# A projection with the contraction outermost, modulation products by 512 columns, and sums in column groups, in a one-core decoder step

## The chip, the core and the metric

The kernel runs on one core of one Trainium2 chip. The metric is the device time of one execution in microseconds, as the median of several runs. The engines meant below are PE (TensorE, matrix products), DVE (VectorE), ACT (ScalarE), POOL (GpSimd) and SP (SyncE, which here only issues DMAs).

## The reference

One decoder layer for a prompt of 256 tokens and 8 samples of 4 new tokens (288 token columns in all). The part that the change touches:

```
mod = (silu(c) @ w_ada + b_ada)            # 1024 x 6144, for 9 condition vectors
sh1, sc1, g1, sh2, sc2, g2 = mod
h = x * (1 + sc1) + sh1
qa, ka, va, qb, kb, vb, ga, gb = split(h @ w_in)   # 1024 x 5120
... rotary, two attention branches, gates, w_pa, w_pb ...
x = layer_norm(alpha * x + g1 * (merged @ w_o))
h2 = x * (1 + sc2) + sh2                    # then w_up, silu, w_down, layer_norm
```

All is float32. Each large product is done as three products of reduced-precision parts: weights and activations are split into a leading part (`hi`) and a rest (`lo`), and hi·hi, hi·lo and lo·hi are added in PSUM.

## The kernel before, in words

Features lie on partitions, and the 288 tokens are columns. A **unit** is 128 output features of one weight matrix: eight contraction blocks, three matmuls each, 24 matmuls of 288 columns into one PSUM bank (`unit_mm`). Two units share one weight load, 1 MB in one of three slots of a ring (`raw`, `RAW = 3`; transfer number n goes to slot n mod 3). ACT copies half a slot to `w_hi` (`split_hi`), DVE subtracts to get `w_lo` (`split_lo`), both four halves ahead of PE (`AHEAD = SPLIT = 4`). SP issues the transfers in order, and `free_slot(n)` makes it wait for what was in the slot: for a projection weight until its last `w_lo` half is made (`lo_ready`), for a piece of `w_ada` until PE has multiplied it (`ada_used`), since that one is read by PE straight from the ring.

A piece of `w_ada` is 256 columns with all eight contraction blocks (`ada_mm`, eight matmuls of 32 x 256 placed in four column groups of PE). Its product is copied by ACT to a row buffer (`ada_rows`), turned by PE (`ada_turn`) and added to the bias by DVE (`ada_add`).

**Opening:** eight pieces (shift and scale of the first sublayer) through the ring, then `h` is formed on DVE and split. **Mixing stage:** twelve rounds c = 0 to 11. In the ring the weights of round c are followed by one piece of `w_ada`; on PE the piece comes ahead of the two units of its round, and its turn behind them. The units alternate between two PSUM banks. After unit nb, ACT evicts the bank and then makes `w_hi` of half nb + 4; DVE shuffles the bank for the rotary embedding (which frees it, `acc_free`) and then makes `w_lo` of half nb + 4. PE waits for `acc_free` of the bank before it starts the next unit there. All these queues are in order.

Then key and value tiles are turned to token-major, the cached keys of the samples are transposed with three gate units between (`keys_turn`, `gate`), attention runs with the other gate units as filler, then `w_pa`/`w_pb`, `w_o`, LayerNorm, `w_up`, `w_down`. LayerNorm's sums are 16 products with a 128 x 128 matrix of 1/1024 (`ones_mm`), of xT and of its square, twelve of them between or behind the `w_o` units of the first six blocks and four at the end.

Of the kernel before, what the change touches and what calls it, by code (L numbers as in the profile page):

```python
# [36 lines left out]
SPLIT = 4  # L37
N_ADA0 = 8
MIX0 = N_ADA0
GATE0 = MIX0 + 24  # L40
# [75 lines left out]
C_END = C_SEL + SAMPLE  # L116


def constants():
# [12 lines left out]
    c[:, C_EPS] = EPS  # L132
    b, h, t = row_of(np.arange(128))
# [12 lines left out]
KV_PLACES = 7  # L146
# [10 lines left out]
ADA_FIRST = (0, 4, 1, 5, 2, 6, 3, 7)  # L157


def ada_chunk(n):  # L160

    if n < MIX0:
        return ADA_FIRST[n]
    if n < GATE0:
        return N_ADA0 + (n - MIX0) // 2 if (n - MIX0) % 2 else None
# [17 lines left out]
MIX_N = 12  # L183
# [27 lines left out]
def gate_slot(g):  # L211

    return ([12, 13, 14, 15, 24, 25, 26, 27, 28, 29, 30, 31, 16, 17, 22, 23])[g]
# [61 lines left out]
def build(nc, x_prompt, x_sample, cache_a, cache_rows, cache_b, page_table, c_prompt, c_sample, w_ada, b_ada, w_in,  # L275
# [24 lines left out]
    kvin, _ = sb("kvin", [128, 2, 6, 256])  # L300
# [7 lines left out]
    rowbuf, _ = sb("rowbuf", [128, 3, 256])  # L308
# [3 lines left out]
    rows, _ = sb("rows", [64, 128])  # L312
# [27 lines left out]
    k_early, _ = sb("k_early", [128, 6, 256], F32, o_qkvg + 24 * TOK * 4)  # L340
    k_late, _ = sb("k_late", [128, 6, 256], F32, o_tmp + 3 * 768 * 4)
# [3 lines left out]
    shift, _ = sb("shift", [128, TOK], F32, o_tmp)  # L345
    off_mean, _ = sb("off_mean", [128, TOK], F32, o_tmp + TOK * 4)
# [6 lines left out]
    st6, _ = sb("st6", [128, 3, 4, 6])  # L353
# [19 lines left out]
    c_zero, c_ready, ada_used, first_in = sem("c_zero"), sem("c_ready"), sem("ada_used"), sem("first_in")  # L373
# [21 lines left out]
    centred = sem("centred")  # L395
    centred_s, h2s_ready, pool_step, x1_scaled = (sem(n) for n in ("centred_s", "h2s_ready", "pool_step", "x1_scaled"))
# [29 lines left out]

    def raw_half(n_static_slot, hh, by_rows):

        if by_rows:
# [3 lines left out]
    def kv_place(b, kind):  # L433

        return (b % 4, b // 4) if kind == 0 else V_PLACE[b]

    def kv_tiles(b, kind, tile, n=1):

        place, _ = kv_place(b, kind)
        if place < 5:  # L440
# [11 lines left out]
    def part(t, slot, by_rows):  # L452
        if by_rows:
# [3 lines left out]
    def split_hi(act, nb, slot4, rslot, hh, need, by_rows=False):  # L457

        if isinstance(nb, int) and nb == 0:
            act.wait_ge(first_in, 16)  # L460
        else:
            act.wait_ge(raw_in[rslot], need)
# [10 lines left out]
    def halves(first, last):  # L473

        out = []
        for n in range(first, last):
            by_rows = PAB0 <= n < WO0 or n >= DOWN0
# [17 lines left out]

    PAB_BANK = (0, 1, 6, 3)
# [4 lines left out]
    SUMS_AFTER = {5: (0, 1), 6: (2, 3, 4), 7: (5,)}  # L501
# [1397 lines left out]
```

## Time and profile before

| | |
|---|---|
| runs, us | 570.57, 571.57, 565.12 (median 570.57) |
| profiled execution, us | 565.61 |
| its span on the core, us | 564.0 |
| granted TensorE clock, mean of the span | 0.966 |
| PE busy, us | 515.1 of 564.0 |
| bytes moved | 116.77 MB |

The profiled execution is about 5 us under the median of the three runs. Busy time of PE is the time in which a matmul is in flight. A granted clock of 1.00 is 2.4 GHz and 0.50 is 1.2 GHz. The kernel has a stretch of opening (to 42 us), the mixing stage (to 147 us), attention and gates (to about 280 us), output projection and LayerNorm (to about 335 us) and the feed-forward part.

### The profile page before, as it was taken

How to read it: one execution, taken by the hardware profiler on the slowest of the kernel's cores; microseconds unless marked ns; L12 is line 12 of the kernel's file. 1: busy time of each engine (PE TensorE's matmuls, PEld its weight loads, DVE VectorE, ACT ScalarE, POOL GpSimd, SP SyncE). 2: the span in 40 equal slices, each digit the busy share in tenths (PEclk: the TensorE clock that was granted, in tenths of full speed). 3: DMA queues.
4: the chain of work that ended last, by engine and by line, in shares of the span. 5: the costliest groups of instructions: out<-in, count | busy, mean ns of one | idle time of the engine just before them, and what ended most of it. 6: DMA issues, size and time to landing. Idle time of an engine off the chain costs nothing.

```text
span 564.0 us, 10305 instructions
## 1 busy us (share of the span) xinstructions
PE 515.1 (91%) x4047; PEld 473.5 (84%) x4047; DVE 289.5 (51%) x560; ACT 223.9 (40%) x376; POOL 91.9 (16%) x127
## 2 busy tenths in 40 slices
PE   3767999999999989999989979999999999999990
PEld 1537899989877979897889869999999999999980
DVE  0074657556643453354486586536555554335356
ACT  1053233334334454255543445455444434333311
POOL 1000113002860000000145052601111100000005
PEclk9977899999999999999899989999999999999995
DMA  8998599988086982183443363899776754354002
GB/s 278 336 286 261 186 368 343 344 274 278 8 279 204 287 285 76 47 278 131 150 150 116 110 224 113 286 333 305 248 272 221 254 191 159 128 200 163 24 1 84
DMA packets 96718, 116.77 MB, mean 207 GB/s; under 512 B 3595, under 2 KB 87755, under 8 KB 96164
## 3 DMA queue, kind: packets, MB, share of 16 engines
q1 hardware_dynamic: 94788, 102.74, 56.2%
q0 software_dynamic: 1888, 13.44, 6.7%
q8 instruction: 30, 0.49, 0.4%
q14 instruction: 12, 0.10, 0.1%
HBM read 112.89 MB, written 13.57 MB: 224 GB/s over the span
## 4 chain that ended last, share of the span: by engine, by line
PE 78%; DMA 11%; DVE 5%; ACT 2%; issue 1%; POOL 1%; SPq 1%; POOLq 0%; ACTq 0%; DVEq 0%
PE psum L654 20%; PE psum L656 19%; PE psum L655 19%; PE psum L679 4%; DMA raw<-in_w_in 4%; DMA raw<-in_w_up 3%; DMA raw<-in_w_ada 3%; PE psum L775 3%; PE psum L900 2%; PE psum L687 1%; PE psum L886 1%; PE psum L844 1%; PE psum L975 1%; PE psum L853 1%; PE psum L787 1%
## 5 line engine op out<-in xcount | busy, mean ns | idle before, releaser
L654 PE MATMUL psum<-act_hi,w_hi 128*128 128x288 f32 x736 | 224.1, 304 | 10.7 <-DVE act_lo L1625 3.9
L470 DVE TENSOR_TENSOR w_lo<-raw,w_hi 128x1024 fp32r<-128x1024 f32 x118 | 146.6, 1243 | 168.2 <-ACT w_hi L465 168.0
L655 PE MATMUL psum<-act_lo,w_hi 128*128 128x288 f32 x736 | 219.2, 298 | 0.0
L656 PE MATMUL psum<-act_hi,w_lo 128*128 128x288 f32 x736 | 218.5, 297 | 0.0
L465 ACT ACTIVATE w_hi<-raw 128x1024 fp32r<-128x1024 f32 x118 | 124.1, 1056 | 141.2 <-PE psum L656 92.6
L654 PEld LDWEIGHTS psum<-act_hi,w_hi 128*128 128x128 f32 x736 | 140.2, 191 | 19.0 <-issue 10.4
L655 PEld LDWEIGHTS psum<-act_lo,w_hi 128*128 128x128 f32 x736 | 140.5, 191 | 0.2
L656 PEld LDWEIGHTS psum<-act_hi,w_lo 128*128 128x128 f32 x736 | 140.7, 191 | 0.0
L654 PE MATMUL psum<-f_hi,w_hi 128*128 128x288 f32 x176 | 52.4, 298 | 0.6 <-DVE f_t L1663 0.6
L655 PE MATMUL psum<-f_lo,w_hi 128*128 128x288 f32 x176 | 51.9, 295 | 0.0
L656 PE MATMUL psum<-f_hi,w_lo 128*128 128x288 f32 x176 | 51.8, 294 | 0.0
L679 PE MATMUL psum<-raw,c_z 128*32 128x256 f32 x384 | 31.8, 460 | 7.0 <-DMA raw<-in_w_ada 7.0
L1767 POOL TENSOR_TENSOR qkvg<-qkvg,cst 128x288 f32 (+1 forms) x16 | 16.3, 1016 | 120.9 <-ACT qkvg L1134 120.9
L654 PEld LDWEIGHTS psum<-f_hi,w_hi 128*128 128x128 f32 x176 | 33.0, 187 | 0.9 <-issue 0.8
L656 PEld LDWEIGHTS psum<-f_hi,w_lo 128*128 128x128 f32 x176 | 33.1, 188 | 0.0
L655 PEld LDWEIGHTS psum<-f_lo,w_hi 128*128 128x128 f32 x176 | 33.0, 188 | 0.0
L1801 POOL TENSOR_TENSOR qkvg<-qkvg,gated 128x288 f32<-128x288 f32 x8 | 8.4, 1081 | 121.1 <-DVE gated L1580 121.1
L679 PEld LDWEIGHTS psum<-raw,c_z 128*32 128x32 f32 x384 | 11.5, 124 | 16.0 <-DMA raw<-in_w_ada 8.2
L1852 POOL DMA_DIRECT2D out<-in_cache_kv_a x24 | 11.7, 488 | 78.1 <-PE psum L656 76.5
L687 PEld LDWEIGHTS psum<-cst,rowbuf 128*128 128x128 f32 x96 | 15.2, 223 | 9.2 <-issue 4.9
L1298 ACT ACTIVATE silu_t<-psum 128x288 f32<-128x288 f32 x22 | 9.0, 408 | 33.3 <-PE psum L656 33.3
L1858 POOL TENSOR_TENSOR y_tok<-y_tok,ln_rows 128x512 f32<-128x512 f32 x2 | 3.4, 1702 | 104.3 <-ACT y_tok L1336 104.3
(180 smaller groups left out, 567.2 us busy)
## 6 DMA issues: line engine op xcount, KB each, us to landing
raw<-in_w_ada SPq DMA_DIRECT2D x24, 1024.0 KB, 7.4
raw<-in_w_up SPq DMA_DIRECT2D x22, 1024.0 KB, 6.2
raw<-in_w_in SPq DMA_DIRECT2D x19, 1024.0 KB, 7.2
raw<-in_w_down SPq DMA_DIRECT2D x10, 1024.0 KB, 4.9
out<-in_cache_kv_a POOLq DMA_DIRECT2D x16, 504.0 KB, 6.3
raw<-in_w_o SPq DMA_DIRECT2D x4, 1024.0 KB, 4.9
kvin<-in_cache_kv_a SPq DMA_DIRECT2D x8, 256.0 KB, 3.3
kvin<-in_cache_kv_b SPq DMA_DIRECT2D x16, 128.0 KB, 3.8
```

What stands on the lines that cost most here:

```text
L465: nc.scalar.activation(part(w_hi, slot4, by_rows), raw_half(rslot, hh, by_rows), ACT.Copy).then_inc(hi_ready, 1)
L470: nc.vector.tensor_tensor(part(w_lo, slot4, by_rows), raw_half(rslot, hh, by_rows), part(w_hi, slot4, by_rows).bitcast(F32), ALU.subtract) ...
L654: nc.tensor.matmul(out, hi_l, hi_r, start=start, stop=False, skip_group_check=True)
L655: nc.tensor.matmul(out, hi_l, lo_r, start=False, stop=False, skip_group_check=True)
L656: return nc.tensor.matmul(out, lo_l, hi_r, start=False, stop=stop, skip_group_check=True)
L679: mm = nc.tensor.matmul(psum[q:q + 32, bank, 0:256], c_z[:, k, :], raw8(slot)[:, k, :], start=(k < 4), stop=(k >= 4), skip_group_check=True)
L687: mm = nc.tensor.matmul(psum[:, ada_bank(i), 256 + 9 * hh:256 + 9 * hh + 9], rowbuf[:, i % 3, 128 * hh:128 * hh + 128], cst[:, C_ADA:C_ADA ...
L775: mm = nc.tensor.transpose(psum[:, bank, col:col + nr], kv_tiles(b, 0, tile)[0:nr, 0, 128 * hp:128 * hp + 128], cst[0:nr, 0:nr])
L900: mm = nc.tensor.matmul(psum[:, 6, E * i:E * i + E], prbT[:, u % 2, 128 * n:128 * n + 128], tok[:, kb, 1, 256 * g + E * h:256 * g + E * h ...
L1298: nc.scalar.activation(silu_t[:, q, :], psum[:, q, 0:TOK], ACT.Silu).then_inc(silu_ready, 1)
L1767: nc.gpsimd.tensor_tensor(block_at(qkvg, blk), block_at(qkvg, blk), cst[:, C_COS:C_COS + TOK], ALU.mult).then_inc(cos_done, 1)
L1852: pool.dma_start(kv_sample[g][bass.ds(b, 1), 0:BUF[g] - DEC_T, :], cache_rows[g][bass.ds(b, 1), DEC_T:BUF[g], :]).then_inc(moved, 16)
```

## The change

- **Opening.** `w_ada` is now taken by 512 columns and half the contraction (four matmuls of 32 x 512, one per column group), 1 MB as before; two such parts make a chunk, so there are 12 chunks and 24 parts. The first eight parts have five buffers of their own (`ada_s`), outside the ring. The order of chunks is 0, 2, 1, 3: shift and scale of the first 512 features come first.
- **First six units.** The units of blocks 12 to 17 (the values of the first branch) are computed together in six banks, contraction block by contraction block (`first_mm`: 18 matmuls for a block k). Their weights come as four transfers of two contraction blocks by 768 columns (0.75 MB) in the ring. Blocks 0 to 3 need only the first half of `h`, and the parts of chunks 1 and 3 are multiplied between them.
- **Mixing stage.** Nine rounds are left (`MIX_C`) and twelve parts of `w_ada`, in the order `MIX`: round 0, part, round 1, part, round 2, two parts, and so on by threes. PE takes rounds and parts in the order of the ring. Turns come once for two parts (96 turning products in all, as before).
- **Samples' keys.** Five of eight samples' keys are loaded before they are needed and not four, `keys_turn` runs in regular order with one `sample_scores` and one gate unit after turns 5, 9 and 13; gates take other slots.
- **LayerNorm sums.** For six of eight blocks the sums are made with a 128 x 32 matrix of 1/32 in four column groups (`quarter_sums`), evicted by ACT and DVE (`part_sum`), and gathered with two `ones_mm` (`gather_quarters`). Two blocks keep the old form.

```
+MIX_C = (0, 1, 2, 3, 4, 5, 9, 10, 11)
+MIX = [item for i in range(9) for item in [("w", i)] + [("a", m) for m in range(4 * i // 3, 4 * (i + 1) // 3)]]
+MIX0 = 4
+GATE0 = MIX0 + len(MIX)
+ADA_ORDER = (0, 2, 1, 3, 4, 5, 6, 7, 8, 9, 10, 11)
+START_BUF = (0, 1, 2, 3, 4, 0, 1, 2)
+    ROWS_AT = {2: 4, 3: 5, 5: 6, 6: 7, 8: 8}
...
             if m >= 0 and ada_chunk(m) is not None:
-                sp.wait_ge(ada_used, N_ADA_BEFORE[m] + 1)
+                sp.wait_ge(ada_used, N_ADA0 + N_ADA_BEFORE[m] + 1)
...
+        load_start(0)
...
+        load_start(1)
+        sp.dma_start(x_tok[:, 0:2, :], x_prompt.rearrange("a (t p) d -> p (a t) d", p=128)).then_inc(x_in, 16)
+        sp.dma_start(x_tok[0:SAMPLE, 2, :], x_sample.rearrange("b t d -> (b t) d")).then_inc(x_in, 16)
+        load_start(2)
+        load_start(3)
+        load_first(0)
+        load_first(1)
+        for q in range(4, N_ADA0):
+            load_start(q)
+        load_first(2)
+        load_first(3)
...
+    def first_mm(pe, k):
+
+        pe.wait_ge(lo_ready, k + 1)
+        pe.wait_ge(h_lo, k + 1)
+        for q in range(FIRST_N):
+            c = 128 * q
+            mm = mm3(psum[:, q, 0:TOK], w_hi[:, k % SPLIT, c:c + 128], w_lo[:, k % SPLIT, c:c + 128], act_hi[:, k, :], act_lo[:, k, :],
+                     k == 0, k == KT - 1)
...
-        for c in range(MIX_N):
+        first_mm(pe, 0)
+        first_mm(pe, 1)
+        ada_start(pe, 4)
+        first_mm(pe, 2)
+        ada_start(pe, 5)
+        first_mm(pe, 3)
+        ada_turn(pe, 2)
+        ada_start(pe, 6)
+        ada_start(pe, 7)
+        ada_turn(pe, 3)
+        for k in range(4, KT):
+            first_mm(pe, k)
+
+        to_turn = None
+        for n in range(MIX0, GATE0):
+            kind, m = MIX[n - MIX0]
+            if kind == "a":
+                ada_ring(pe, n)
+                if m % 2:
+                    to_turn = 4 + m // 2
+                continue
             for hh in range(2):
-                u = 2 * c + hh
-                if c >= 1 and hh == 0 or u == 1:
-                    ada_mm(pe, MIX0 + 2 * c + 1)
-                if c >= 1:
-                    pe.wait_ge(acc_free[hh], c)
-                unit_mm(pe, u, u % SPLIT, hh, h_lo if u == 0 else None)
-            ada_turn(pe, N_ADA0 + c)
+                nb = H_MIX + 2 * m + hh
+                pe.wait_ge(acc_free[hh], m + 1)
+                unit_mm(pe, nb, nb % SPLIT, hh)
+                if to_turn is not None:
+                    ada_turn(pe, to_turn)
+                    to_turn = None
...
+        for m, c in enumerate(MIX_C):
             for hh in range(2):
-                nb = H_MIX + 2 * c + hh
-                if c >= 1 and hh == 0:
-                    ada_rows(N_ADA0 + c)
+                nb = H_MIX + 2 * m + hh
+                if hh == 0 and ROWS_AT.get(m) is not None:
+                    ada_rows(ROWS_AT[m])
                 if c in ROPED:
                     act.wait_ge(half_used, nb + 1)
                     nc.scalar.activation(qkvg[:, 2 * c + hh, :], psum[:, hh, 0:TOK], ACT.Copy).then_inc(evicted, 1)
                 if nb + AHEAD < H_GATE + 2:
                     hi_static(act, nb + AHEAD)
...
+        def quarter_sums(first, last):
+            pe.wait_ge(squared, last)
+            for bank, src in ((4, xT), (5, qkvg[:, 8:16, :])):
+                for q in range(last - first):
+                    mm = nc.tensor.matmul(psum[32 * q:32 * q + 32, bank, 0:TOK], cst[:, C_W32:C_W32 + 32], src[:, SUM_ORDER[first + q], :],
+                                          start=(first == 0), stop=(first > 0), skip_group_check=True)
+            mm.then_inc(quarters_done, 1)
```

How the change moves instructions at three places of the mixing stage. In these rows `in_w_in` is a projection weight (1 MB, one round), `in_w_ada` a part of `w_ada`, and the bracket names the semaphores that the instruction waits for.

**SP, the ring in the mixing stage.** Before, from the second piece of the stage on (the `in_w_ada` of round 0):

```order
L525 DMA raw<-in_w_ada 128x8x256 [waits ada_used]
L525 DMA raw<-in_w_in 128x8x256 [waits ada_used]
L525 DMA raw<-in_w_ada 128x8x256 [waits lo_ready]
L525 DMA raw<-in_w_in 128x8x256 [waits ada_used]
L525 DMA raw<-in_w_ada 128x8x256 [waits lo_ready]
```

Now, from round 0 on:

```order
L547 DMA raw<-in_w_in 128x8x256 [waits lo_ready]
L547 DMA raw<-in_w_ada 128x4x512 [waits lo_ready]
L547 DMA raw<-in_w_in 128x8x256 [waits lo_ready]
L547 DMA raw<-in_w_ada 128x4x512 [waits lo_ready]
L547 DMA raw<-in_w_in 128x8x256 [waits ada_used]
L547 DMA raw<-in_w_ada 128x4x512 [waits lo_ready]
L547 DMA raw<-in_w_ada 128x4x512 [waits ada_used]
L547 DMA raw<-in_w_in 128x8x256 [waits lo_ready]
```

The fifth of these is the weight of round 2. It goes to the slot of the part behind round 0, as before the change; its wait is on that part's product.

**PE, rounds 0 and 1 and the part between them.** Before (a round: the piece, then its two units, then the turn):

```order
L679 MATMUL psum<-raw,c_z 32x256 [waits ada_mod,raw_in2]
L679 MATMUL psum<-raw,c_z 32x256 x7
L654 MATMUL psum<-act_hi,w_hi 128x288 [waits lo_ready,acc_free0]
...
L654 MATMUL psum<-act_hi,w_hi 128x288 [waits lo_ready,acc_free1]
...
L687 MATMUL psum<-cst,rowbuf 128x9 [waits ada_row]
```

Now, from the second unit of round 0 to the second unit of round 1:

```order
L693 MATMUL psum<-act_hi,w_hi 128x288 [waits lo_ready,acc_free1]
...
L714 MATMUL psum<-raw,c_z 32x512 [waits ada_mod,raw_in2]
L714 MATMUL psum<-raw,c_z 32x512 x3
L693 MATMUL psum<-act_hi,w_hi 128x288 [waits lo_ready,acc_free0]
...
L693 MATMUL psum<-act_hi,w_hi 128x288 [waits lo_ready,acc_free1]
```

The part whose product frees the slot for round c + 2 stood ahead of the units of round c and now stands behind them.

**ACT, from unit 0 of round 0 on.** L1226 evicts a unit, L486 makes `w_hi` of the half that is four ahead, L1184 is the row copy that a turn waits for.

```order
L1226 ACTIVATE qkvg<-psum 128x288 [waits half_used]
L486 ACTIVATE w_hi<-raw 128x1024 [waits half_used,raw_in2]
L1226 ACTIVATE qkvg<-psum 128x288 [waits half_used]
L486 ACTIVATE w_hi<-raw 128x1024 [waits half_used,raw_in2]
L1226 ACTIVATE qkvg<-psum 128x288 [waits half_used]
L486 ACTIVATE w_hi<-raw 128x1024 [waits half_used,raw_in2]
L1226 ACTIVATE qkvg<-psum 128x288 [waits half_used]
L486 ACTIVATE w_hi<-raw 128x1024 [waits half_used,raw_in2]
L1184 ACTIVATE rowbuf<-psum 128x512 [waits ada_used]
```

The alternation of evictions and halves is that of before, and so is the row copy's place behind both halves of the next round's weight (here round 3's, the last two L486). But the turn that needs the copy stood on PE behind both units of its round, and now stands behind the first.

## Rows read from the trace of the kernel before

**Rows 1.** The page's first part: busy us, share of span, instructions.

```profile
PE 515.1 (91%) x4047; PEld 473.5 (84%) x4047; DVE 289.5 (51%) x560; ACT 223.9 (40%) x376; POOL 91.9 (16%) x127
```

**Rows 2.** Stages: length, busy us per engine, PEclk granted clock, DMA share, GB/s.

```profile
14.00:42.20 28.20, 18.83 (x152) 12.55 (x151) 10.80 (x35) 8.08 (x19) 0.00 (x0) 0.85 1.00 312
42.20:56.00 13.80, 10.66 (x66) 9.68 (x67) 5.96 (x9) 4.48 (x8) 0.81 (x1) 0.75 0.81 262
...
70.00:112.00 42.00, 42.00 (x360) 38.98 (x359) 25.27 (x54) 14.45 (x23) 8.68 (x8) 1.00 1.09 352
112.00:126.00 14.00, 12.97 (x115) 11.52 (x114) 6.83 (x14) 4.67 (x6) 0.00 (x0) 1.00 0.87 279
126.00:147.30 21.30, 21.30 (x180) 20.09 (x179) 12.94 (x34) 6.43 (x10) 8.20 (x29) 1.00 0.60 196
```

**Rows 3.** Timeline of PE, opening: start us, duration, operation, idle before.

```profile
21.37 1.93 PE L679 MATMUL psum<-raw,c_z 128*32 128x256 f32 x16 [3.75 <-DMA raw<-in_w_ada]
...
42.21 0.61 PE L654 MATMUL psum<-act_hi,w_hi 128*128 128x288 f32 x1 [3.56 <-DVE w_lo L470]
...
55.57 1.02 PE L687 MATMUL psum<-cst,rowbuf 128*128 128x9 f32 x4 [3.13 <-ACT rowbuf L1105]
```

**Rows 4.** Chain that ended last, in time, start us and duration: one period.

```profile
66.63 1.00 PE psum L679 x16
...
74.56 1.00 PE psum L679 x16
```

**Rows 5.** The same chain where it leaves PE.

```profile
107.36 9.53 DMA raw<-in_w_in
116.91 1.07 ACT w_hi L465
118.00 1.23 DVE w_lo L470
119.23 0.38 DVE qkvg L1439
```

**Rows 6.** The same chain at the end of the mixing stage.

```profile
147.25 0.27 PE psum L755 x2
```

**Rows 7.** Timeline of DVE at the same place.

```profile
118.00 1.23 DVE L470 TENSOR_TENSOR w_lo<-raw,w_hi 128x1024 fp32r<-128x1024 f32 x1 [5.45 <-ACT w_hi L465]
```

**Rows 8.** DMA issues: count, KB each, median us from issue to landing.

```profile
raw<-in_w_in SPq DMA_DIRECT2D x19, 1024.0 KB, 7.2
raw<-in_w_down SPq DMA_DIRECT2D x10, 1024.0 KB, 4.9
```

**Rows 9.** Groups by line from 60 to 150 us: busy us, mean ns.

```profile
L470 DVE TENSOR_TENSOR w_lo<-raw,w_hi 128x1024 fp32r<-128x1024 f32 x20 | 24.4, 1218 | 23.4 <-ACT w_hi L465 23.4
L465 ACT ACTIVATE w_hi<-raw 128x1024 fp32r<-128x1024 f32 x20 | 20.8, 1054 | 32.1 <-DMA raw<-in_w_in 31.9
...
L1412 DVE STREAM_SHUFFLE rope_t<-psum 128x288 f32<-128x288 f32 x14 | 6.9, 491 | 0.1
...
L1105 ACT ACTIVATE rowbuf<-psum 128x256 f32<-128x256 f32 x10 | 3.8, 376 | 0.1
```

**Rows 10.** PE by the microsecond around two long idles: busy, PEclk.

```profile
55.00:56.00 1.00, 0.43 (x2) 0.50 1.10 349
60.00:61.00 1.00, 1.00 (x6) 0.50 0.88 282
...
333.00:334.00 1.00, 1.00 (x6) 0.50 1.10 369
335.00:336.00 1.00, 0.65 (x5) 1.00 0.23 74
```

**Rows 11.** The chain at the sums of LayerNorm.

```profile
315.56 2.91 PE psum L975 x12
```

**Rows 12.** What PE waited for from 100 us on: us, times, longest.

```profile
PE psum L775 <- DVE kc_a L1467: 1.5, 2, 0.8
...
PE psum L775 <- DVE tok L1461: 0.9, 1, 0.9
```

More of the change, by code:

```diff
@@ L452, in part @@
     def part(t, slot, by_rows):
+        if by_rows == "first":
+            return t[:, slot, 0:FIRST_COLS]
         if by_rows:
@@ L457, in split_hi @@
     def split_hi(act, nb, slot4, rslot, hh, need, by_rows=False):
[L459 to L462, printed above, removed]
+        act.wait_ge(raw_in[rslot], need)
         if not isinstance(nb, int) or nb >= SPLIT:
@@ L1022, in first_up_pair @@
                 for q in range(3):
-                    wh, wl = part(w_hi, q, False), part(w_lo, q, False)
+                    wh, wl = (part(w, (H_UP + q) % SPLIT, False) for w in (w_hi, w_lo))
                     mm = mm3(psum[:, UP_BANK[q], 0:TOK], wh[:, k, :], wl[:, k, :], act_hi[:, k, :], act_lo[:, k, :], k == 0, k == KT - 1)
@@ L1259, in _ @@
             if m == 7:
+                act.wait_ge(quarters_done, 2)
+                nc.scalar.activation(part_sum[:, 0, :], psum[:, 4, 0:TOK], ACT.Copy).then_inc(quarters_x, 1)
                 hi_static(act, H_UP + 3)
@@ L1382, in modulate_pair @@
             modulate_prompt(qkvg, xT, 2 * p + 1, 0, 1, h_ready)
[L1384 to L1401 removed]
+        ada_add(0)
@@ new lines, in _ @@
+        for j in range(2):
+            dve.wait_ge(turned_x, j + 3)
+            V.tensor_copy(xT[:, 4 * j:4 * j + 4, 128:256],
+                          psum[:, 3 + j, :].rearrange("p (k c) -> p k c", c=128)).then_inc(x_ready_dve, 1)
+        dve.wait_ge(turned_x, 5)
+        V.tensor_copy(xT[:, :, PROMPT:TOK], psum[:, 0, 0:256].rearrange("p (k c) -> p k c", c=SAMPLE)).then_inc(x_ready_dve, 1)
+        dve.wait_ge(x_ready_act, 2)
+        dve.wait_ge(x_ready_dve, 3)
+        ada_add(1)
+        modulate_pair(0)
@@ L1402, in _ @@
+        lo_static(dve, 0)
+        rest_of(qkvg, 0, h_hi, h_lo)
+        rest_of(qkvg, 1, h_hi, h_lo)
+        modulate_pair(1)
+        lo_static(dve, 1)
+        rest_of(qkvg, 2, h_hi, h_lo)
+        rest_of(qkvg, 3, h_hi, h_lo)
+        lo_static(dve, 2)
+        lo_static(dve, 3)
+        ada_add(2)
+        ada_add(3)
+        modulate_pair(2)
         modulate_pair(3)
-        lo_static(dve, H_MIX)
+        lo_static(dve, 4)
+        rest_of(qkvg, 4, h_hi, h_lo)
+        rest_of(qkvg, 5, h_hi, h_lo)
@@ L1404, in _ @@
+        lo_static(dve, 5)
         rest_of(qkvg, 6, h_hi, h_lo)
         rest_of(qkvg, 7, h_hi, h_lo)
-        for nb in range(H_MIX + 1, H_MIX + AHEAD):
+        for nb in range(6, 11):
             lo_static(dve, nb)
+        for q in (1, 3, 5):
+            if q < 5:
+                dve.wait_ge(first_done, q + 1)
+            else:
+                dve.wait_ge(half_used, KT)
+            V.tensor_copy(qkvg[:, FIRST_BLK + q, :], psum[:, q, 0:TOK]).then_inc(acc_free[1] if q == 1 else v_free, 1)
```

376 lines of the change are left out of this document (196 added, 180 removed).

## The prediction, written before the change was run

> **What bounds the kernel now.** I began with busy time: PE has a matmul in flight for 515.1 of 564.0 us [rows 1], so only some 49 us are idle and the rest of any gain is clock or work. The table of stages shows where they lie. In the opening PE is idle for 9.4 us between 14 and 42 and for 3.1 us up to 56, with a granted clock of 0.85 and 0.75, while the DMA engines are full until 42; from 70 to 112 PE is never idle, the clock is 1.00, and the DMA engines are full too, at 352 GB/s; from 126 to the stage's end PE is full and the DMA engines are not [rows 2]. The timeline of PE gives the opening's waits: the fourth piece of `w_ada` at 21.37, the first projection unit at 42.21, and a turn at 55.57 [rows 3]. A round of the mixing stage takes 74.56 - 66.63 = 7.93 us [rows 4], and the stage ends at 147.25 [rows 6].
>
> The view that decides is the chain of waits at 107 us [rows 5]. PE has just multiplied the piece that frees a slot; the weight of a round *two rounds on* is issued at 107.36 and lands 9.53 us later; ACT makes its `w_hi`, DVE its `w_lo`, and only then does DVE empty the bank of a unit that PE finished long before. DVE's own timeline shows it: it sits 5.45 us idle in front of that `w_lo`, and the eviction (`qkvg` in [rows 5]) stands right behind it [rows 7]. So a late weight does not wait for its own round. Through the in-order queues of ACT and DVE it stops PE one round earlier, at the next unit that wants the bank. Here the transfer was issued at the start of a round and had a whole round and half of the next to hide in; Of the 14 us from 112 to 126 PE lost 1.03 [rows 2].
>
> **Part 1, opening and first six units (a gain).** Ahead of the third and fourth `w_ada` transfers the same bytes go as before, so the fourth arrives near 21.4 us. Its product takes 1.93 us at that clock [rows 3]. Row copy of 512 columns (0.376 us for 256 [rows 9], so about 0.6), eight turning products (the four in [rows 3] took 1.02, so 1.9), one add, and two feature blocks modulated and split, about 3: the first matmul of a unit can start near 29 us against 42.21. Then 144 matmuls, a round's 48 of which take 7.93 less 1.35 of other work, so 6.5 us per 48 and 19.5 us; four parts of `w_ada` 4.0; two sets of turns 1.5; a wait for the second half of `h`, since its turn comes directly behind its products and four blocks must be modulated before block 4 can start, about 5; and two stretches at half clock, 4.5. Sum 63.5 us. This estimate may be off by 3 us either way.
>
> **Part 2, the mixing stage without waits.** Nine rounds of 6.5, twelve parts of 1.0 (the products' columns are as many as before), five turns of 0.7: 74. It would end at 137.5, 9.7 us ahead of 147.25. Were this all, the change would pay.
>
> **Part 3, where the waits go.** The part of `w_ada` whose product frees the slot for round c + 2 has moved behind round c's two units. The weight of round c + 2 is therefore issued 6.5 us later than before, at the start of round c + 1, and the second unit of round c + 1 needs the bank that DVE empties only behind `w_lo` of that weight. Take 5.3 us from issue to landing: between the median of 4.9 of a 1 MB transfer with little beside it (`w_down`) and 7.2 of those in the full stage, nearer to the former since the stalls leave the queue empty [rows 8]. The three kinds of place, each counted from the end of the product that frees the slot:
>
> - A weight issued first: 0.15 + 5.3 + `w_hi` 1.05 + `w_lo` 1.22 + shuffle 0.5 [rows 9] = 8.2; PE has one unit, 3.2, to do. Idle 5.0.
> - A weight behind a part of `w_ada` freed at the same moment (round 3): 3.0 more for 1 MB at 352 GB/s, and the turn in the round before needs the row copy, which stands on ACT behind both halves: 0.6 + 8.3 + 1.05 + 0.4 + 1.05 + 0.6 less 0.4 that overlaps = 11.6, less the 3.2. Idle 8.4.
> - A weight behind a part issued 1 us before it (round 4): the same less 1.0. Idle 7.4.
>
> The order repeats by three rounds, so rounds 2 to 8 and the first gate weight make 3 x 5.0 + 3 x 8.4 + 2 x 7.4 = 55 us of idle. Nothing covers it: on PE all that stands between are units behind the same banks, and the `w_ada` products in between are themselves what SP waits for, so no gap shortens another. The Trainium skill (DMA: Bandwidth & Descriptors, Anatomy of one DMA) gives a transfer a fixed 2.0 us and its bytes at 436 GB/s. By that page 1 MB would land in an estimated 4.4 us, each gap would be 0.9 shorter and the time about 620.
>
> **Part 4, the clock.** After an idle of 3.13 us PE ran at 0.50 from 55 to past 60 us; after one of 3.5 us at 331 it was at 0.50 beyond 333 and back at 335 [rows 3, 10]. So 3.1 to 5.6 us at half clock follow a long idle, and half of that is lost, 1.6 to 2.8. Eight gaps of 5 us and more: 13 to 22, I take 18. The Trainium skill (TensorE: Matmul & The Clock Gate, What's actually happening) says for modelling that the ramp's cost is under 1% of a typical kernel's span. By that this term would be at most 6 us and the time about 615. The rows show the drop at each long idle, so I keep 18.
>
> **Part 5, small ones.** LayerNorm sums: twelve products of two blocks' kind cost 2.91 per six [rows 11], 5.8 for twelve. In four groups they need four passes; eight products of 256 columns in four groups took 1.00 [rows 4], so a pass of 288 is about 0.56: 2.2, plus two gathering products 0.97. Gain 2.6, if the evictions hide under the last `w_o` unit (3.2 us, two copies of 0.5). If the groups did not overlap it would be a loss of 1. Samples' keys: of the waits there (1.5 and 0.9 us [rows 12]) most go, 2 us; the moved loads lie in a stretch that will have DMA time to spare. Gate slots and sigmoids: the same number of operations on ACT, in a stretch that PE bounds: nothing.
>
> **Sum:** 147.25 becomes 63.5 + 74 + 55 + 18 = 210.5, that is +63; less 4.6. Against the profiled execution: 565.6 + 58.6 = 624. That execution is 5 us under the median of the three runs, so I forecast 627.
>
> **The rivals.**
> - *The clock holds.* Units between the gaps may be dense enough for it to recover at once. For it: 331 us, back after 3 us. Then only some 3 of the 18 us remain: 609 to 612.
> - *Loads in front.* Masks (1.3 MB) and four sets of cached keys (0.7 MB each) are issued in the same stage; the transfer in [rows 5] took 9.5 us with such loads ahead. For five weights 4.2 us more each is 21: 648. Against: here they are issued behind the weight of their round, and the gaps let them drain.
> - *Faster after all.* If the waits of part 3 do not reach PE, only parts 1, 2 and 5 act: 565.6 - 9.7 - 4.6 = 551. The point that decides is 3.2 us: the weight would have to be landed and split within one unit after its issue. The fastest median is 4.9 for the landing alone, so this needs a wait in the code to be other than I read it.
> - *A third of the waits.* Were only the first of the three kinds real, 15 us of idle and 5 of clock would eat the gain: 571, no change.
>
> **How the numbers follow.** Forecast case (627, own range 612 to 640) 0.72; the clock holds 0.11; loads in front 0.10; faster 0.05; no change 0.02. Lower end: landing at 4.9 (-3), clock term at 3 (-15), opening 3 better, the profiled rather than the median level (-5): 601. Upper end: landing at 7.1 for all (+14), clock at 22 (+4), and a little of the loads in front: 648. About 1 in 8 is left outside. Two runs of this kernel differ by up to 1%, which is what I take a measurement to tell from no change. Faster by over 1%: 0.05; within 1%: 0.02; slower: 0.93.
>
> **What the changed profile would show.** Right, part 1: the first 288-column matmul near 29 us and the last of the six units between 60 and 67. Part 3: PE's idle time between 64 and 210 us near 55, with its releasers DVE's shuffle of a bank and ACT's row copy, in gaps of 5 to 8 us at the second unit of rounds 1, 4 and 7 and at the turns; ACT's `w_hi` idle before it by DMA `in_w_in` far over the 31.9 us of now; DMA share near 0.6. Part 4: PEclk of about 0.7 to 0.8 in that stage. Part 5: the sums 2.6 us shorter, and attention and feed-forward unchanged in length. Wrong: a mixing stage without idle on PE, or a stage that ends before 180 us.

## The result and the profile after

| | before | after |
|---|---|---|
| median of the runs, us | 570.68 (565.12 to 571.57, 4 runs) | 632.31 (631.36 to 632.69, 4 runs) |
| ratio | | 1.11, 95% interval 1.103 to 1.117 |
| span of the profiled execution, us | 564.0 | 630.9 |
| granted clock, mean | 0.966 | 0.928 |

The change costs 11%. The forecast was 627, with a range of 601 to 648.

The first part of the page (busy us, share of the span, instructions) has more busy time on PE for fewer instructions than [rows 1]:

```profile
PE 533.1 (84%) x3859; PEld 485.3 (77%) x3859; DVE 294.2 (47%) x548; ACT 222.0 (35%) x370; POOL 95.5 (15%) x127
```

Matmuls that take longer in flight are a matter of the clock, not of a wait. The table of windows (length, PE, PEld, DVE, ACT, POOL busy, PEclk, DMA share, GB/s) says where. Its three rows are the mixing stage from the end of the first six units, the token turns, and the samples' keys:

```profile
63.40:214.46 151.06, 97.51 (x569) 84.82 (x569) 51.57 (x105) 24.60 (x39) 27.68 (x41) 0.79 0.47 159
214.46:224.18 9.72, 8.01 (x61) 7.27 (x58) 7.83 (x19) 4.33 (x16) 3.02 (x1) 0.82 0.36 116
224.18:269.30 45.12, 44.89 (x408) 37.04 (x406) 19.70 (x41) 20.26 (x40) 10.27 (x16) 1.00 0.80 253
```

In [rows 2] the middle of that stage had no idle time, a clock of 1.00 and the DMA engines full. Now PE is idle for 151.06 - 97.51 = 53.6 us of it, the clock is 0.79 and the DMA engines are busy for less than half. No engine is full: what is left is a chain. PE's timeline has the eight gaps (start us, duration, operation, in brackets the idle time before it and who ended it):

```profile
79.03 0.51 PE L693 MATMUL psum<-act_hi,w_hi 128*128 128x288 f32 x1 [4.73 <-DVE rope_t L1516]
...
96.10 1.87 PE L728 MATMUL psum<-cst,rowbuf 128*128 128x9 f32 x8 [7.72 <-ACT rowbuf L1184]
```

and so on at 116.60 (7.75), 132.98 (4.50), 151.73 (9.40), 171.16 (7.14), 187.66 (4.60) and 205.05 (7.71): three at the second unit of rounds 1, 4 and 7, and five at the turns. The view of waits, for PE between 62 and 216 us (what it waited for: us in total, times, longest), sums them by releaser:

```profile
PE psum L728 <- ACT rowbuf L1184: 39.7, 5, 9.4
PE psum L693 <- DVE rope_t L1516: 13.8, 3, 4.7
```

The chain of waits (start us, duration) over the third and fourth gap answers to [rows 5]:

```profile
106.18 7.56 DMA raw<-in_w_in
...
115.11 0.94 ACT w_hi L486
116.06 0.50 ACT rowbuf L1184
116.60 1.88 PE psum L728 x8
118.47 0.44 PE psum L693
...
123.23 0.24 PE psum L694
...
123.83 0.14 PE psum L694
...
124.10 1.04 PE psum L714 x8
125.15 5.03 DMA raw<-in_w_in
130.21 1.06 ACT w_hi L486
131.29 1.17 DVE w_lo L491
132.46 0.48 DVE rope_t L1516
132.98 0.40 PE psum L693
```

Read it from 124.10. PE multiplies a part of `w_ada` (L714), which frees the slot. SP issues the weight of the round after next into it at once, and it lands 5.03 us later. ACT splits it, DVE takes its low part, and only then does DVE's shuffle free the bank that PE wants for its next unit. In the gap before (from 106.18), the copy of a modulation row stands on ACT behind both halves of that gap's own late weight. ACT's own wait for projection weights (`raw<-in_w_in`) from 63 to 214 us grew from the 31.9 us of [rows 9]:

```profile
L486 ACT ACTIVATE w_hi<-raw 128x1024 fp32r<-128x1024 f32 x17 | 17.9, 1052 | 114.9 <-DMA raw<-in_w_in 114.9
```

The transfers themselves are no slower than those of [rows 8]. They only start later. The three late weights that are issued first land 5.03 to 5.25 us after their issue, the five behind a part of `w_ada` 7.56 to 8.31. In two of these five gaps (at 116.60 and 151.73) SP also reads page numbers for about 1.1 us between the part and the weight, and the weight goes out 1.5 us after the product that freed its slot; no run here takes that away alone. The median of all weights (count, KB each, median us from issue to landing):

```profile
raw<-in_w_in SPq DMA_DIRECT2D x17, 1024.0 KB, 7.3
raw<-in_w_down SPq DMA_DIRECT2D x10, 1024.0 KB, 5.0
```

The half clock behind a gap is seen in windows of 2 us (columns as above) after the one that ends at 151.73:

```profile
154.00:156.00 2.00, 2.00 (x10) 2.00 (x9) 1.85 (x9) 0.00 (x0) 0.00 (x0) 0.50 0.00 0
156.00:158.00 2.00, 2.00 (x11) 2.00 (x11) 0.44 (x1) 0.00 (x0) 0.00 (x0) 0.58 0.00 0
158.00:160.00 2.00, 2.00 (x18) 0.96 (x21) 0.00 (x0) 0.00 (x0) 0.00 (x0) 1.00 0.00 0
```

What that costs stands in the chain above: a matmul of 288 columns takes 0.24 us at half clock (123.23) and 0.14 at full clock (123.83). Read by the microsecond, the half clock lasts 5.9 to 7.2 us behind each of the five gaps at turns and 3.4 to 4.2 us behind the three at banks.

### The profile page after: what moved, and what is told of

It reads as the page before. It is cut to its first block, busy times and chain, and to the rows that moved or that the text cites. A ratio compares the mean times of both kernels' runs of the same rounds, so it can differ in the third digit from the quotient of the medians.

```text
span 630.9 us, 9903 instructions
## 1 busy us (share of the span) xinstructions
PE 533.1 (84%) x3859; PEld 485.3 (77%) x3859; DVE 294.2 (47%) x548; ACT 222.0 (35%) x370; POOL 95.5 (15%) x127
## 4 chain that ended last, share of the span: by engine, by line
PE 73%; DMA 12%; DVE 5%; ACT 3%; issue 3%; SPq 2%; POOL 1%; POOLq 0%; DVEq 0%; ACTq 0%
PE psum L693 20%; PE psum L694 18%; PE psum L695 18%; DMA raw<-in_w_in 10%; PE psum L714 3%; PE psum L728 3%; ACT w_hi L486 2%; PE psum L849 2%; PE psum L965 2%; DMA ada_s<-in_w_ada 1%; DVE w_lo L491 1%; PE psum L951 1%; DMA kvin<-in_cache_kv_b 1%; PE psum L909 1%; PE psum L918 1%
## 5 line engine op out<-in xcount | busy, mean ns | idle before, releaser
L491 DVE TENSOR_TENSOR w_lo<-raw,w_hi 128x1024 fp32r<-128x1024 f32 (+1 forms) x120 | 149.6, 1248 | 237.5 <-ACT w_hi L486 237.3
L693 PE MATMUL psum<-act_hi,w_hi 128*128 128x288 f32 x736 | 232.5, 316 | 25.0 <-DVE rope_t L1516 13.8
L694 PE MATMUL psum<-act_lo,w_hi 128*128 128x288 f32 x736 | 227.0, 308 | 0.0
L695 PE MATMUL psum<-act_hi,w_lo 128*128 128x288 f32 x736 | 225.9, 307 | 0.0
L486 ACT ACTIVATE w_hi<-raw 128x1024 fp32r<-128x1024 f32 (+1 forms) x120 | 124.6, 1041 | 222.7 <-DMA raw<-in_w_in 122.7
L693 PEld LDWEIGHTS psum<-act_hi,w_hi 128*128 128x128 f32 x736 | 148.2, 201 | 37.6 <-DVE rope_t L1516 14.5
L694 PEld LDWEIGHTS psum<-act_lo,w_hi 128*128 128x128 f32 x736 | 148.3, 202 | 0.1
L695 PEld LDWEIGHTS psum<-act_hi,w_lo 128*128 128x128 f32 x736 | 148.1, 201 | 0.0
L728 PE MATMUL psum<-cst,rowbuf 128*128 128x9 f32 x96 | 18.1, 318 | 42.6 <-ACT rowbuf L1184 42.6
L1184 ACT ACTIVATE rowbuf<-psum 128x512 f32<-128x512 f32 x12 | 7.1, 593 | 36.8 <-PE psum L714 36.8
```

The source lines that it names most:

```text
L486: nc.scalar.activation(part(w_hi, slot4, by_rows), raw_half(rslot, hh, by_rows), ACT.Copy).then_inc(hi_ready, 1)
L491: nc.vector.tensor_tensor(part(w_lo, slot4, by_rows), raw_half(rslot, hh, by_rows), part(w_hi, slot4, by_rows).bitcast(F32), ALU.subtract) ...
L693: nc.tensor.matmul(out, hi_l, hi_r, start=start, stop=False, skip_group_check=True)
L694: nc.tensor.matmul(out, hi_l, lo_r, start=False, stop=False, skip_group_check=True)
L695: return nc.tensor.matmul(out, lo_l, hi_r, start=False, stop=stop, skip_group_check=True)
L728: mm = nc.tensor.matmul(psum[:, ADA_BANK[i], 9 * hh:9 * hh + 9], rowbuf[:, i % 2, 128 * hh:128 * hh + 128], cst[:, C_ADA:C_ADA + 9], start ...
```

## The experiments

Theory: a part of `w_ada` that PE multiplies behind its round frees its slot one round too late, and the late weight stops PE through the in-order queues of ACT and DVE. Each gap is then followed by some microseconds at 1.2 GHz. The main rivals: a bank or buffer is short whatever the order; ACT's copy is the wait by itself; the clock is only a symptom beside the chain.

The ratios below are to the kernel before, timed beside each set of experiments; its median was 570.7 us beside the changed kernel and 566.1 to 567.4 beside the experiments. A difference between medians of two sets can therefore be off by some 4 us, and the traces are used for its parts.

### 1. TensorE's order alone put back

```
-    ROWS_AT = {2: 4, 3: 5, 5: 6, 6: 7, 8: 8}
+    ROWS_AT = {1: 4, 2: 5, 4: 6, 5: 7, 7: 8}
...
             if kind == "a":
-                ada_ring(pe, n)
-                if m % 2:
-                    to_turn = 4 + m // 2
                 continue
+            to_turn = None
+            n2 = n + 1
+            while n2 < GATE0 and MIX[n2 - MIX0][0] == "a":
+                ada_ring(pe, n2)
...
```

> The changed kernel with TensorE's order of the mixing stage alone put back: a part of w_ada that follows a unit in the order of the ring is multiplied ahead of that unit, as the kernel before did it; units by 512 columns, the opening, the sums and the order of the keys stay changed. My theory is that the gaps of 4.5 to 9.4 us before the second half of units 1, 4 and 7 and before the turns (53.6 us in all), and the half clock behind them (98 us of busy TensorE where I sized 74), come of that order: TensorE has nothing left while a key's transfer of 5.0 to 7.6 us lands and is split. Then this kernel's gaps in the mixing stage sum to under 10 us, no stretch of it is at 1.2 GHz, the first token turn is near 143 us of the span (it was 214.5, and 147.3 before the change) and the time is 632 - 71 = 561 us, under the 570.7 of the kernel before. The rival says that a bank or a buffer, not the order of the parts, is short: where two parts follow each other in the ring, the second lacks its key as before. Then only one kind of gap goes and the other two (8 and 7 us, five of them) stay: 600 to 612 us.

In the part that is not shown, the parts of `w_ada` behind a unit in the ring are multiplied ahead of it, and `to_turn` is set there. `ROWS_AT` moves ACT's row copies one round earlier with them.

Measured: 556.62 us median, 0.983 of the kernel before (0.979 to 0.988). The stage from the end of the six units to the first token turn, and the token turns:

```profile
64.00:141.83 77.83, 75.88 (x569) 64.42 (x569) 48.92 (x103) 25.83 (x40) 20.12 (x22) 1.00 0.93 322
141.83:148.06 6.23, 6.23 (x59) 5.65 (x58) 5.31 (x20) 3.85 (x15) 6.00 (x20) 1.00 0.07 15
```

The same 569 matmuls as in the changed kernel: 2.0 us idle in place of 53.6, 75.9 us busy in place of 97.5, the DMA engines full again. The token turns are back at 6.2 us. All five gaps at turns went together with the three at banks, so the second part of a pair does not lack its weight ("key" in the texts above is a projection weight) either, and the rival falls. With nothing else undone, the kernel is faster than before the change. This run also splits the loss of the stage by measurement: 73.2 us, of which 51.6 are idle time and 21.6 are clock.

### 2. ScalarE's and VectorE's order alone changed

```
-                if hh == 0 and ROWS_AT.get(m) is not None:
-                    ada_rows(ROWS_AT[m])
...
-                if nb + AHEAD < H_GATE + 2:
-                    hi_static(act, nb + AHEAD)
+                if hh == 1 and ROWS_AT.get(m + 1) is not None:
+                    ada_rows(ROWS_AT[m + 1])
+                if nb + 3 < H_GATE + 2:
+                    hi_static(act, nb + 3)
```

(and the same `nb + 3` for `lo_static` on DVE)

> The changed kernel with only ScalarE's and VectorE's order changed in the mixing stage: a key's half is split three halves ahead instead of four, and the copy of a modulation row out of its PSUM bank stands ahead of the split on ScalarE, not behind it. TensorE's order stays as changed. One theory is that the gaps are waits behind a split: the row copy and the rotated tokens that TensorE lacks stand on ScalarE and VectorE behind the split of a key whose transfer has yet to land (the chain reads transfer 7.56, split 0.94, copy 0.50, then TensorE's turn). Then the gaps of 53.6 us fall to some 10 us, the clock holds, and the time is 632 - 44 - 15 = 573 us, between 568 and 580. The rival is that TensorE would be short of the weights in any case, because a key that is asked for when its buffer is freed lands 5 to 7.6 us later, and that the copies only stand nearest in the row of waits: then the gaps change their name (to the split halves) and keep their sum, and the time is 615 or more.

Measured: 578.41 us, ratio 1.024 (1.018 to 1.030). Windows of its stage:

```profile
61.20:159.66 98.46, 80.17 (x569) 68.95 (x569) 52.38 (x102) 25.18 (x40) 18.03 (x20) 0.93 0.72 244
```

18.3 us idle, and 4.3 us of clock. Here the weights are asked for just as late, by the same products. But a unit whose bank waits behind the split of a half three ahead is one unit later in PE's order, and two thirds of the idle time go. (The edit also moves the row copy ahead of the split. By experiment 9 that alone is worth some 14 us of the 54 that this kernel gains.) So the transfer is late for ACT's queue long before it is late for PE. The rest, 18 us, is what TensorE's order costs beyond that.

### 3. The gaps filled with unused matmuls

```
+        def filler(n):
+            pe.wait_ge(v_free, 4)
+            for _ in range(n):
+                nc.tensor.matmul(psum[:, 4, 0:TOK], act_hi[:, 0, 0:128], act_hi[:, 0, :], start=True, stop=True,
+                                 skip_group_check=True)
...
+                if hh == 1 and m in (1, 4, 7):
+                    filler(30)
...
                 if to_turn is not None:
+                    filler(48)
                     ada_turn(pe, to_turn)
```

> The changed kernel with matmuls of 288 columns whose result nobody reads put where TensorE stands idle in the mixing stage: 30 ahead of the second half of units 1, 4 and 7 (3.6 us at 0.12 us each), and 48 ahead of each turn (5.8 us). They fill most of each gap and end nothing sooner. They tell the two parts of the loss apart. My theory has 24 us of it as half clock after the gaps (98.0 us of busy TensorE against the 74 of the sum): filled, the clock holds, the work behind each gap is done in full speed, and the time is 632 - 20 = 612 us (607 to 618). The rival: the chain through the gap is transfer, split and copy, and the work behind the gap at half clock lies beside the next transfer, so that a faster TensorE only waits longer: the clock is up in the records and the time stays within 5 us of 632.

Measured: 619.02 us, ratio 1.095 (1.089 to 1.101). The same stage, first all of PE, then the unused matmuls alone:

```profile
63.66:201.01 137.35, 126.74 (x900) 114.08 (x899) 50.81 (x108) 24.61 (x39) 24.56 (x40) 0.95 0.52 176
```

```profile
63.66:201.01 137.35, 44.75 (x330) 43.94 (x330) 0.95 0.52 176
```

The other matmuls take 126.74 - 44.75 = 82.0 us where they took 97.5 (and 75.9 at full clock). Idle time and fillers together are 55.4 us where the idle time alone was 53.6. So adding work to PE made the stage 13.7 us shorter: of the 21.6 us of clock, 15.5 came back, and all but 1.8 of that ended the stage sooner. The rival, in which a faster PE only waits longer, is refuted. The time fell by 13 us and not by 20: 0.5 to 1.9 us of each gap stayed open, and the clock came to 0.95 only.

### 5. The copy of a row ahead of one split

```
-                if hh == 0 and ROWS_AT.get(m) is not None:
-                    ada_rows(ROWS_AT[m])
...
+                if hh == 1 and ROWS_AT.get(m + 1) is not None:
+                    ada_rows(ROWS_AT[m + 1])
                 if nb + AHEAD < H_GATE + 2:
```

> The changed kernel with one move alone: on ScalarE the copy of a modulation row stands ahead of the splits of the halves (the split stays four halves ahead, TensorE's order stays as changed). In the changed kernel five of the eight gaps, 39.7 of 53.6 us, end with that copy. My theory is that the copy only stands nearest in a row of waits behind the same late weight: with it gone TensorE does its turn in time and then waits for VectorE's shuffle of the bank, which stands behind the low half of the same weight. The five gaps lose little (the copy and what ScalarE did between, 1 to 2 us each), their releaser becomes the shuffle, and the time is 632 - 5 to 12, near 624. The rival takes the releaser's name at its word: five gaps of 39.7 us vanish with the clock they cost, 632 - 40 - 10 = 582 or less.

Measured: 627.19 us, ratio 1.109 (1.103 to 1.115). By the ratio alone it cannot be told from the changed kernel's 1.110; the gaps can, and they sum to 49.5 us. So the time agrees with my theory, but one part of the reason failed: the releaser of the five gaps is still ACT's copy. It stood behind two splits of the late weight and now stands behind one. The five gaps are 6.76, 7.51, 8.00, 5.88 and 6.73 us where they were 7.72, 7.75, 9.40, 7.14 and 7.71, 4.8 us less in all. (The second lost only 0.24: its weight took 8.27 us to land where it took 7.56. The "1.0 to 1.4 us each" of the next expectation holds for the other four.)

### 9. The copy ahead of both splits

```
+                if hh == 0 and ROWS_AT.get(m + 1) is not None:
+                    ada_rows(ROWS_AT[m + 1])
```

(in the place of the lines of experiment 5)

> The changed kernel with one move alone: on ScalarE the copy of a modulation row stands ahead of both splits of the late weight (in the fifth experiment it stood behind the first of them, and its five gaps lost 1.0 to 1.4 us each, about one split of 1.05 us, and kept ScalarE's copy as their releaser). My theory: the copy no longer waits for the weight, TensorE turns in time, and the wait moves to the next bank, which VectorE frees behind the low half of the same weight: transfer, 1.05, 1.22 and 0.5 us where it was transfer, 1.05, 1.05, 0.6 and then the turn of 0.9. The gaps' releaser is VectorE's shuffle in all eight, their sum is above 45 us, and the time is 627 - 5 = 622 (617 to 628). The rival: the copy was the wait, and the five gaps vanish: under 590.

Measured: 618.12 us, ratio 1.090 (1.083 to 1.096), as expected. The profiled execution took 628.7 us, over that median, so its chain and its releasers are read here and not its lengths:

```profile
100.65 1.04 PE psum L714 x8
...
103.22 8.67 DMA raw<-in_w_in
111.91 1.06 ACT w_hi L486
113.00 1.17 DVE w_lo L491
114.17 0.48 DVE rope_t L1516
114.69 0.61 PE psum L693
```

The turns wait no more. All eight gaps now end with DVE's shuffle; in the view of waits PE has none for the copy any more:

```profile
PE psum L693 <- DVE rope_t L1516: 50.7, 8, 8.0
```

Where a wait for the copy was taken away, the wait for the bank behind the same weight took its place. The 39.7 us put down to the row copy in the changed kernel are true and a poor guide: with that wait removed, some 14 us of the 62 lost came back.

### 6. Half the bytes of the weights

```
-                load(n, n % RAW, w_in_v[:, :, 256 * c:256 * c + 256], raw8(n % RAW))
+                kt = KT if m < 2 else 4
+                load(n, n % RAW, w_in_v[:, 0:kt, 256 * c:256 * c + 256], raw8(n % RAW)[:, 0:kt, :])
```

> The changed kernel, but the weights of rounds 2 to 8 of the mixing stage are loaded by their first four contraction blocks alone, 0.5 MB instead of 1 MB each; the other four blocks are whatever the slot held. Everything else, the splits of all eight blocks too, is as before. If the gaps hold the transfer's time from its issue on, each of the seven that these weights end is shorter by the time of 0.5 MB, 1.4 to 1.5 us at the 352 GB/s of the full stage, and the time is 632 - 10 = 622 us. If a fixed part makes most of the 5 us of a transfer, it is 632 - 3 or less; if the weight was queued behind other loads, the gaps keep their length.

This kernel leaves out half of the contraction of these weights. Measured: 618.93 us, ratio 1.095 (1.088 to 1.102), 13.4 us less than the changed kernel. The gaps sum to 42.3 us, 11.3 less. The last one, which waits for a gate weight of full size, is 7.64 us where it was 7.71; the other seven lost 1.6 us each on average, from 0.65 to 2.51. The transfer in the chain that took 5.03 us now reads:

```profile
117.13 3.44 DMA raw<-in_w_in
120.60 1.06 ACT w_hi L486
121.69 1.17 DVE w_lo L491
122.85 0.47 DVE rope_t L1517
```

So each gap holds the transfer from its issue on, and on average the bytes left out count fully (1.4 to 1.5 us were expected). The three gaps at banks stand with no other load ahead of the weight, so queueing does not make the gaps; behind a part of `w_ada` it makes them longer, by the 2.3 to 3.3 us between the two kinds of landing above.

### 4. The column-group sums alone, in the kernel before

```
-    SUMS_AFTER = {5: (0, 1), 6: (2, 3, 4), 7: (5,)}
+    IN_QUARTERS = 6
...
+            if m == 6:
+                quarter_sums(0, 4)
+                quarter_sums(4, IN_QUARTERS)
+        gather_quarters()
         sums(6)
```

> The kernel before with one part of the change alone: six of the eight tiles of each LayerNorm sum go by a quarter of the columns each, four at once into one bank, and are gathered by one matmul more per sum. My theory: the stretch from the first sum to the end of the sums' part is shorter by 2.4 to 2.6 us (24.5 to 22.1 in the changed kernel), the rest is equal, and the time is 570.6 - 2.5 = 568 us, a ratio of 0.9956. The rival: what the sums save is lost in the two copies and the gathering that the LayerNorm now waits for: 570 to 572 us.

Measured: 560.78 us, ratio 0.992 (0.988 to 0.996). The chain at the sums, and PE's timeline where `w_up` starts:

```profile
295.52 0.97 PE psum L979 x4
...
309.27 2.06 PE psum L993 x24
```

```profile
324.13 0.37 PE L658 MATMUL psum<-act_hi,w_hi 128*128 128x288 f32 x1 [3.51 <-DVE act_lo L1652]
```

From the shift sums to `w_up` it takes 324.13 - 295.52 = 28.6 us. In the kernel before the same sums start at 299.88 and `w_up` at 331.05, 31.2 us. The part saves 2.6 us. By the ratio the time fell by 4.6 us, with an interval from 2 to 7. Of the two profiles' difference of 7.4 us, 3.0 lie ahead of the first token turn (at 144.08 and not 147.10), which this edit does not touch; I take that for the spread of the kernel's runs.

### 7. Both orders together

The edits of experiments 1 and 2 in one kernel.

> TensorE's order of the mixing stage put back as in the first experiment, and ScalarE's and VectorE's as in the second (a split three halves ahead, the row copy first). With the first alone 2 us of idle are left in the stage, with the second alone 18. My theory: the order on TensorE is what frees the slots, so nothing is left for the second to gain; and a half that is split one unit later has less in hand where the DMA engines are full (0.92 of the stage in the first experiment), so it may cost 0 to 4 us: 556.6 + 2 = 559, between 556 and 562. The rival: the last 2 us of idle go, and with them some VectorE waits later on: 554.

Measured: 559.24 us, ratio 0.986 (0.982 to 0.991), as expected. PE now waits in the stage for the parts of `w_ada` themselves, 5.4 us in six places. The second order cures nothing that the first leaves, and the first alone is not worse.

### 8 and 10. Unused matmuls in the gaps that remain

```
+        pe.wait_ge(ada_mod, 1)
+        keep_warm(20, 6, ones, cst[:, 0:128])
         first_mm(pe, 0)
...
+        pe.wait_ge(ada_mod, 3)
+        keep_warm(25, 6, act_hi[:, 0, 0:128], act_hi[:, 0, :])
         for k in range(4, KT):
...
+            keep_warm(9, 4, ones, part_sum[:, 0, :])
             pe.wait_ge(z_ready, KT)
```

(experiment 10: 5 in the place of the 9)

> The first experiment's kernel with matmuls whose result nobody reads in its three remaining gaps where TensorE then runs at 1.2 GHz: 20 of 128 columns in the 3.0 us ahead of the first unit, 25 of 288 columns in the 4.1 us ahead of the second half of h, 9 in the 2.9 us ahead of w_up. Behind these gaps the first experiment shows 1.2 GHz from 28.5 to 33, from 51.6 to 57 and from 321.9 to 326.7 us, half of which is lost: 2.3 + 2.8 + 2.4 = 7.5 us. If that clock goes with the idle and is on the path that sets the end, the time is 556.6 - 7 = 550 us (548 to 553). The rival: TensorE is not alone on the path there, since the next blocks of h or of h2 are made by VectorE while it runs slowly; then it only waits longer, and the time is within 2 us of 556.6.

> The kernel of the eighth experiment with 5 unused matmuls in its third gap instead of 9. There the 9 took 4.4 us (0.24 us for each of their 18 passes), 1.3 more than the gap of 2.9 ahead of w_up, and from the turn of the last modulation rows to the end it gained 0.4 us of the 2.4 expected. With 5 they take 2.4 us and end inside the gap: 1.2 us off, so 551.7 against 552.9. The rival: VectorE, which is 0.91 busy there with the blocks of h2, sets the pace and not TensorE: no difference, 552.9.

Measured: 552.88 us, ratio 0.976 (0.971 to 0.981), at the upper end of what I expected, and with the shorter third filler 555.97 us, ratio 0.983 (0.978 to 0.988), slower where I expected 1.2 us less. The intervals of these two overlap, and so do those of each and of experiment 1 (0.979 to 0.988).

### 11 and 12. Experiments 1 and 8 side by side

> The kernel of the first experiment once more, beside the next run on the same chip in the same rounds, since the eighth and tenth (0.976 and 0.983 of the kernel before) and the first (0.983) came from different chips and differ by less than their intervals. Expected as before: 0.983 of the kernel before, near 557 us.

> The kernel of the eighth experiment beside that of the first. My theory: the unused matmuls give back the half clock of the opening, 5 us by the stage's length in the two traces (113.3 and 107.6 us from the first unit to the first token turn), so this one is 4 to 6 us under the one beside it, a ratio near 0.976. The rival: the difference in the traces was the transfers' and not the clock's, and the two are within 2 us.

Measured: 554.34 us, ratio 0.977 (0.973 to 0.981), against 555.91 us, ratio 0.980 (0.976 to 0.985) with the fillers. The clock did what was wanted. The stretch behind the second gap, first without and then with fillers:

```profile
49.00:60.00 11.00, 10.65 (x70) 10.68 (x71) 6.55 (x10) 4.56 (x7) 0.00 (x0) 0.85 0.64 200
```

```profile
49.00:60.00 11.00, 10.31 (x80) 9.94 (x83) 7.22 (x10) 4.69 (x7) 0.00 (x0) 1.00 0.69 209
```

In the profiled executions the stretch from the first unit to the first token turn was 8.6 us shorter with fillers (114.9 and 106.3), and the span 4.8 us shorter (556.0 and 551.2). Only 4.0 of the 8.6 lie in the first six units, where the fillers stand (34.4 and 30.4 us); the rest lies in the mixing stage, where none stand and the version without them waits twice, 1.8 and 1.6 us. And its profiled execution was the slowest of its six, while the other was the second fastest. The medians of the six runs each show none of it. My theory of 4 to 6 us is not confirmed. One profile of each kernel cannot carry a difference that is as large as the spread of its runs (553.3 to 557.6 and 552.5 to 559.4). Whether the fillers gain anything stays open.

No version is then shown to be better than that of experiment 1: 0.983 and 0.977 of the kernel before in two sets of runs, against 1.11 for the change as it was.

## Why the prediction came out right

**What bounds, and the place.** Right. Between 64 and 210 us the idle time has the two releasers named, in the places named, and the order on TensorE is its cause (experiment 1). The DMA share there was 0.47, under the 0.6 that I had named.

**Part 1, opening.** First matmul expected near 29 us, measured 29.37. The wait for the second half of `h`, sized about 5, was 4.07. Timeline of PE:

```profile
29.37 0.58 PE L693 MATMUL psum<-act_hi,w_hi 128*128 128x288 f32 x1 [3.00 <-DVE act_lo L1465]
...
52.48 0.58 PE L693 MATMUL psum<-act_hi,w_hi 128*128 128x288 f32 x1 [4.07 <-DVE act_lo L1465]
```
The six units end at 63.4 (the part of `w_ada` behind round 0 starts at 69.85, less 6.45 for the round), expected 63.5.

**Part 2, the stage without waits.** Sized 74 us; experiment 1 measures 75.9 busy and 2.0 idle. Expected end 137.5, measured there 141.83. The gain of the opening was thus 5.3 us (147.1 to 141.8) and not 9.7. The working had five turns at 0.7, and they take 0.96 each, 1.3 us more. A stage with the DMA engines 0.93 busy kept 2 us of waits, where I allowed none. That kernel's six units ended 0.5 later, and 0.6 is spread over the rounds.

**Part 3, idle time.** Sized by kind at 3 x 5.0, 3 x 8.4 and 2 x 7.4 = 55 us. Measured 13.8 for the three of the first kind, 24.8 for the three of the second, 14.9 for the two of the third: 53.6. The base of each, a landing of 5.3 us, was 5.03 to 5.25 in the three of the first kind; with a part in front I had 8.3 and 7.3, measured 7.74 to 8.31 and 7.56 to 7.61. The page numbers that SP reads in two of these gaps were not in the sum. The Trainium skill (DMA: Bandwidth & Descriptors, Anatomy of one DMA — SWDGE (gpsimd) path) would give an estimated 4.4 for the weight issued at 125.15, which took 5.03. Its figures are for transfers that GpSimd issues, and this one is issued by SP; the measurement decides. Halving the bytes took 1.6 us off that transfer, 3.2 us for a MB. By the page's 436 GB/s half a MB is an estimated 1.2 us: here too the trace is above the page.

**Part 4, clock.** Sized 18 us (13 to 22), measured 97.5 - 75.9 = 21.6, the upper end. The number per gap is 2.7 us and not 2.2: behind the five gaps at turns PE was at half clock for 5.9 to 7.2 us, longer than the 5.6 that I had read from [rows 10]. 21.6 us are 3.4% of the span. The Trainium skill (TensorE: Matmul & The Clock Gate, What's actually happening) puts the ramp under 1% of a typical kernel's span, where it tells of a kernel's first matmuls; this kernel paid eight times, and the trace does not agree. Experiment 3 shows that it is time and not only a busy count.

**Part 5.** Sums sized 2.6 us: 2.6 alone (experiment 4), and 2.4 in the changed kernel, from 369.46 to 398.28 us:

```profile
398.28 0.58 PE L693 MATMUL psum<-act_hi,w_hi 128*128 128x288 f32 x1 [2.92 <-DVE act_lo L1734]
```

Samples' keys sized 2 us: 45.1 us (224.18 to 269.3) against 46.2 (153.45 to 199.66), so 1.1.

**What I left out.** The token turns took 9.7 us for 6.3. They begin at full clock, wait 1.7 us for DVE until 218.88, and run at half clock for some 3.4 us behind that. In experiment 1 they took 6.2 without a wait, so these 3.4 us belong to the same cause.

**The sum** of the stage's end is 67.4 us later where 63.3 was expected: waits 1.4 less, clock 3.6 more, the stage itself 1.9 more. With 3.4 for the token turns, and part 5 saving 3.5 in place of 4.6, the 624 worked out against the profile become 632.6; the profiled execution took 632.5. So the errors mostly add up, and the sum was 8.5 us short. The forecast of 627 was only 5.3 us short of the median of 632.3, and that is luck: I had added 3 us since the kernel before was profiled under its median, and the changed kernel was profiled at its own.

**The rivals.** "The clock holds" fell by the trace. "Loads in front" fell: the weight issued at 125.15 with cached keys behind it landed in 5.03 us, and none of the eight late weights took more than 8.31, against the 9.5 of that rival. "A third of the waits" fell: all three kinds of gap are in the trace. "Faster after all" is what experiment 1 is, at 556.6 and 554.3, where that rival had 551: its mechanism needed the parts to be multiplied ahead.

## What to carry to other kernels

With a ring shared by work of two kinds, ask of every consumer that moves which transfer it lets start, and count from that issue to the first instruction that stands behind the transfer's split in any in-order queue, not to its own user: here that was one round earlier. When a list of waits names one releaser for most of the idle time, look at what stands in front of the releaser; taking the named wait alone gave some 14 of 62 us, while taking away its cause gave 76. And price a gap with the half clock behind it: 6.7 us of idle each cost 9.4 us here.

## What the hardware showed that I had not expected

- 330 matmuls more (44.75 us of busy time) made the kernel 13 us faster (632.3 to 619.0) and its mixing stage 13.7 us shorter, because they stood where PE would have been idle.
- In the opening the same trick raised the granted clock of the kernel from 0.965 to 0.983 and shortened the first six units in the trace by 4.0 us, with no gain in the median of the runs (554.3 and 555.9). No run here shows why.
- The half clock behind a gap did not grow with the gap: it lasted 5.9 us behind the longest, of 9.4 us, and 7.0 and 7.2 us behind gaps of 7.1 and 7.7 us.
